# Row sums of a gathered table in one instruction or in two halves, beside GpSimd gathers

## The chip, the cores and the metric

The kernel runs on one core of one Trainium2 chip. The metric is the device time of one execution in microseconds, median of three runs. The profile is one execution taken by the hardware profiler; its times are microseconds from the start of its span.

## The reference

The program is a small language model in float32 for 256 positions of width 1024: a latent-attention layer, a gated-linear-attention layer, each followed by a product-key expert layer ("peer"), and a second block with a convolution, an attention and a mixture of 32 experts. The change touches only the peer layers. For a block of 128 positions each of them does this:

```python
def one_block(xi):                                   # xi: 128 positions x 1024
    q = (xi @ w_query).reshape(B, T, PEER_HEADS, 2, PEER_HALF)
    s = jnp.einsum('bthcd,cnd->bthcn', q, sub_keys).astype(jnp.float32)
    s_top, i_top = lax.top_k(s, PEER_TOPK)           # 16 of 128, twice for each of 8 heads
    ...                                              # the best 16 of the pairs: idx, gate
    u = u_tab[idx]                                   # 8 x 16 rows of 1024 for each position
    h = jax.nn.gelu(jnp.einsum('bthkd,btd->bthk', u, xi).astype(jnp.float32), approximate=False)
    w = (gate * h).astype(xi.dtype)
    return jnp.einsum('bthk,bthkd->btd', w, v_tab[idx])
```

Each position picks 128 rows of the table `u_tab`, and as many of `v_tab`, by the same indices. With two layers and two blocks of positions there are four groups of 128, in all 512 steps that the kernel calls rows: in row n every one of the 128 partitions (positions) has one table row of 1024 numbers of its own.

## The kernel before

A row n goes through five engines. GpSimd issues an indirect DMA (`fetch_u`, L671) that brings the 128 table rows, 512 KB, into one of nine buffers `u_rows`, and another (`fetch_v`, L683) for `v_rows`, also nine buffers. VectorE multiplies the u rows with the normalised activations `px` and sums over the 1024 columns into one column of `hid` (L1025, in `row`); the product itself is written back over the buffer and is not used. The semaphore `u_used` counts these. ScalarE applies gelu to eight columns of `hid` at once (L1522), VectorE multiplies them with the gates (L1033, columns of `wgt`), ScalarE makes of each column of `wgt` a diagonal matrix (L1533), and TensorE multiplies the diagonal with the v rows and adds up in two banks of PSUM (L2005). A last few rows are added by VectorE (L1039).

The order on each engine is written out by hand. `Rows` deals out rows between other work: the stage functions (`mla`, `gla`, `route`) call it at their steps, and a table of row targets says how many rows each engine is to have done by each TensorE job. `row(n)` on VectorE sums row n, and at every eighth row, with an offset of two, asks for the gelu of the eight before: `dve.wait_ge(gelu_ready, n // BLK)`. `row(n)` on ScalarE issues the gelu of a full block of eight, and the diagonal of the row ten before; TensorE follows twelve rows behind (`LAG`). In `route`, VectorE runs the top-k of the next group (L913 to L917, six records for each of sixteen score vectors, then index arithmetic) with rows between. At the same time attention or gated linear attention for the other half of the positions keeps TensorE busy.

GpSimd issues its gathers in one fixed order, u and v by turns. Before u row n it waits until row n - 9 has been summed (`pool.wait_ge(u_used, n - RU + 1)`), before v row n until row n - 9 has been multiplied (`v_used`). So a sum that is late can hold the u gather nine rows on, and all gathers behind it in the queue. Each gather reads its 128 indices from a column of `idx` in SBUF.

The sum at L1025 is one call that becomes two instructions on VectorE: the multiply and sum, and a read of the accumulator into the column of `hid`.

Of the kernel before, what the change touches and what calls it, by code (L numbers as in the profile page):

```python
# [6 lines left out]
P = 128  # L7
# [3 lines left out]
BANK = 512  # L11
# [23 lines left out]
BLK, LAG = 8, 12  # L35
# [179 lines left out]
def summed(n):  # L215

    return n - sum(m < n for m in SHARED)
# [69 lines left out]
def build(nc, a, out):  # L287
    f32, i32, u32 = mybir.dt.float32, mybir.dt.int32, mybir.dt.uint32
    ALU, ACT, AX = mybir.AluOpType, mybir.ActivationFunctionType, mybir.AxisListType
    X = AX.X  # L290
    ctx = ExitStack()
    with ctx:
        def sb(name, shape, dt=f32):
            return ctx.enter_context(nc.sbuf_tensor(name, shape, dt))

        def sem(name):
            return ctx.enter_context(nc.semaphore(name))
# [31 lines left out]
        px = sb("px", [P, 2, D])  # L329
        idx = sb("idx", [P, 2, P], i32)  # L330
        gate = sb("gate", [P, 2, P])
        hid = sb("hid", [P, P])
        gel = sb("gel", [P, P])
        wgt = sb("wgt", [P, P])
        diag = sb("diag", [P, DIAGS, P])
# [125 lines left out]
        u_here = [sem(f"u_here{i}") for i in range(RU)]  # L461
        v_here = [sem(f"v_here{i}") for i in range(RV)]
        u_used = sem("u_used")
        v_used = sem("v_used")
        v_taken = sem("v_taken")
        gelu_ready = sem("gelu_ready")
# [231 lines left out]
        def _(dve):  # L698
# [13 lines left out]
            V_ = nc.vector  # L712
# [304 lines left out]
            def row(n):  # L1017

                if n >= P + LAG and (n - LAG) % P == 0:
                    add_experts((n - LAG) // P - 1)  # L1020
                if n < NU:
                    g, r = n // P, n % P
                    dve.wait_ge(u_here[n % RU], 16 * (n // RU + 1))
                    u = u_rows[:, n % RU, :]
                    V_.tensor_tensor_reduce(out=u, in0=u, in1=px[:, g % 2, :], scale=1.0, scalar=0.0, op0=ALU.mult,  # L1025
                                            op1=ALU.add, accum_out=hid[:, r:r + 1]).then_inc(u_used, 1)
                n -= LAG - LEAD - BLK
                if n >= BLK and n % BLK == 0 and n <= NU:
                    g, r = (n - BLK) // P, (n - BLK) % P
                    c = slice(r, r + BLK)  # L1030

                    dve.wait_ge(gelu_ready, n // BLK)
                    V_.tensor_tensor(wgt[:, c], gel[:, c], gate[:, g % 2, c], ALU.mult).then_inc(wgt_ready, 1)  # L1033
                    if n < NU:
                        return
                    dve.wait_ge(wgt_ready, NU // BLK)
                    for m in SHARED:
                        dve.wait_ge(v_here[m % RV], 16 * (m // RV + 1))
                        V_.scalar_tensor_tensor(h[:, 1, :], v_rows[:, m % RV, :], wgt[:, m % P:m % P + 1], h[:, 1, :],  # L1039
                                                ALU.mult, ALU.add).then_inc(v_taken, 1)  # L1040
                        dve.wait_ge(v_taken, SHARED.index(m) + 1)

            rows_done = Rows(row)

            def add_experts(g):
                t = g % 2

                dve.wait_ge(v_used, summed((g + 1) * P))
                V_.tensor_tensor(h[:, t, :], h[:, t, :], psum[:, 6:8, :].rearrange("p a b -> p (a b)"),
                                 ALU.add).then_inc(experts_added, 1)  # L1050
                dve.wait_ge(experts_added, g + 1)
# [291 lines left out]
        def _(act):  # L1343
# [172 lines left out]
            def row(n):  # L1516

                if n >= BLK and n % BLK == 0 and n <= NU:
                    r = (n - BLK) % P
                    c = slice(r, r + BLK)  # L1520
                    act.wait_ge(u_used, n)
                    A_.activation(gel[:, c], hid[:, c], ACT.Gelu).then_inc(gelu_ready, 1)  # L1522
                n -= LAG - LEAD
                if 0 <= n < NU:
                    if n % BLK == 0:
                        act.wait_ge(wgt_ready, n // BLK + 1)
                    if n in SHARED:
                        return
                    at = summed(n)
                    if at >= DIAGS:  # L1530

                        act.wait_ge(v_used, at - DIAGS + 1)
                    A_.activation(diag[:, at % DIAGS, :], ident[:], ACT.Copy, scale=wgt[:, n % P:n % P + 1]).then_inc(diag_ready, 1)  # L1533

            rows_done = Rows(row)

            def gla(t):
# [772 lines left out]
```

## Time and profile before

| | |
|---|---|
| timed runs | 2536.88, 2541.75, 2551.35 us; median 2541.75 |
| profiled execution | span 2647.6 us, the only time listed for it |
| VectorE, GpSimd busy | 1096.6 us (41%), 1124.9 us (42%) |
| L1025, row sums | 512, 616.4 us, mean 1225 ns |
| L671 and L683, gather issues | 512 each, 566.3 and 554.8 us |
| row sums run | from 152.2 to 1761.8 us |
| gathered data | 536.94 MB of 860.19 MB |

"Busy" is the union of an engine's instruction records; an instruction that waits is not busy. A group in the list of the costliest gives the busy time, the mean duration, and the idle time of the engine just before it with what ended it. For a gather on GpSimd the record is the issue of the DMA, not its transfer. A line of the windows view begins with the stretch and its length; then come the busy time and, in brackets, the number of records of PE, PEld, DVE, ACT and POOL, the granted TensorE clock, the busy share of the DMA engines, and the GB/s that they moved. The timeline gives one line for each instruction: start, length, engine, line, operation, and in square brackets the idle time before it. Records of one engine can overlap by some 0.08 us, since an instruction may begin before the one ahead has quite ended. The profiled span is longer than the timed runs; differences in it are read within the profile.

### The profile page before, as it was taken

The page shows a single profiled execution, that of the slowest core. Times are in us where ns is not written, and L with a number is a line of the kernel's source. Part 1 is how long each engine was busy: PE and PEld are TensorE (multiplying, and loading weights), DVE is VectorE, ACT ScalarE, POOL GpSimd, SP SyncE. Part 2 cuts the span into 40 slices and gives each one's busy share as a digit, 9 for nine tenths or more (in the row PEclk, how much of TensorE's full clock was granted, in tenths as well). Part 3 has the DMA queues.
Part 4 walks back from the last instruction along what each step waited for, and adds up shares of the span by engine and source line. Part 5 has one row for each costly group of instructions (what it writes and reads, how often), then busy time and mean ns, then how long its engine had stood idle before and what let it go on. Part 6 is the DMA issues. An engine that isn't in the chain of part 4 may idle for free.

```text
span 2647.6 us, 21106 instructions
## 1 busy us (share of the span) xinstructions
PE 2024.5 (76%) x7462; PEld 1050.7 (40%) x7462; DVE 1096.6 (41%) x2630; ACT 423.9 (16%) x1107; POOL 1124.9 (42%) x1059
## 2 busy tenths in 40 slices
PE   8937797769888677988775866769999995655664
PEld 5613453325344224434331322225888862222221
DVE  6578538942356764345783544431201230000001
ACT  2312311101311110311110111100112310000000
POOL 0057757775556776565776777750000000000000
PEclk9968899899999899999888999999989997887777
DMA  5379999999989999998999999995653369999996
GB/s 208 112 269 350 341 366 390 360 367 383 381 294 398 357 357 377 397 335 315 363 353 364 355 362 365 362 373 135 146 140 102 132 278 403 426 427 427 427 427 272
DMA packets 228318, 860.19 MB, mean 325 GB/s; under 512 B 26080, under 2 KB 26592, under 8 KB 216432
## 3 DMA queue, kind: packets, MB, share of 16 engines
q0 software_dynamic: 147456, 536.94, 54.0%
q1 hardware_dynamic: 77488, 312.04, 31.2%
q10 hardware_dynamic: 3264, 9.80, 1.0%
q8 instruction: 63, 1.03, 0.2%
q14 instruction: 47, 0.39, 0.0%
HBM read 857.64 MB, written 1.05 MB: 324 GB/s over the span
## 4 chain that ended last, share of the span: by engine, by line
PE 39%; DMA 18%; DVE 17%; POOL 11%; issue 8%; another core or an unknown queue 5%; ACT 2%; SPq 1%; DVEq 0%; ACTq 0%; POOLq 0%
PE psum L1814 12%; PE psum L2005 11%; PE psum L1806 6%; DVE rows L1025 6%; POOL rows L671 5%; POOL rows L683 5%; DMA rows<-in_w_e_gate 5%; DMA rows<-in_peer_v,idx 4%; DMA rows<-in_w_e_down 4%; DMA rows<-in_w_e_up 3%; PE psum L2207 3%; PE psum L2230 1%; SPq L546 1%; DVE work L914 1%
## 5 line engine op out<-in xcount | busy, mean ns | idle before, releaser
L2005 PE MATMUL psum<-rows,diag 128*128 128x512 f32 x2024 | 1009.1, 642 | 375.6 <-ACT diag L1533 168.8
L2005 PEld LDWEIGHTS psum<-rows,diag 128*128 128x128 f32 x2024 | 387.9, 203 | 947.4 <-issue 698.0
L1025 DVE CUSTOM_DVE_ANT_0 rows<-rows,px 128x1024 f32<-128x1024 f32 x512 | 616.4, 1225 | 310.7 <-DMA rows<-in_peer_u,idx 258.7
L671 POOL DMA_INDIRECT rows<-in_peer_u,idx x512 | 566.3, 1106 | 383.6 <-issue 149.0
L683 POOL DMA_INDIRECT rows<-in_peer_v,idx x512 | 554.8, 1084 | 271.7 <-issue 129.3
L1814 PE MATMUL psum<-work,rows 128*128 128x256 f32 (+1 forms) x1664 | 292.8, 337 | 7.9 <-issue 7.1
L1814 PEld LDWEIGHTS psum<-work,rows 128*128 128x128 f32 x1664 | 264.4, 196 | 39.5 <-issue 14.4
L1533 ACT ACTIVATE diag<-ident,wgt 128x128 f32<-128x128 f32 x506 | 167.3, 389 | 397.9 <-DVE wgt L1033 222.4
L2207 PE MATMUL psum<-rows,work 128*32 128x512 f32 x896 | 138.2, 699 | 102.3 <-DMA kept<-in_w_e_up 45.8
L1295 DVE TENSOR_TENSOR work<-kept,psum 128x512 f32<-128x512 f32 x8 | 8.2, 1030 | 426.9 <-PE psum L2207 426.9
L1352 ACT ACTIVATE work<-psum 128x512 f32<-128x512 f32 (+4 forms) x158 | 81.8, 533 | 616.3 <-PE psum L1814 161.1
L1806 PE MATMUL psum<-rows,work 128*128 128x512 f32 x354 | 156.0, 595 | 3.6 <-ACT work L1352 1.9
L694 POOL IOTA work<- 128x256 f32 x1 | 0.3, 345 | 306.4 <-ACT kept L1352 306.4
L2230 PE MATMUL psum<-rows,kept 128*32 128x512 f32 x448 | 75.0, 749 | 71.0 <-DMA kept<-in_w_e_down 40.2
L2207 PEld LDWEIGHTS psum<-rows,work 128*32 128x32 f32 x896 | 39.1, 126 | 195.0 <-issue 194.9
L1806 PEld LDWEIGHTS psum<-rows,work 128*128 128x128 f32 x354 | 67.2, 191 | 88.5 <-issue 85.9
L1522 ACT ACTIVATE gel<-hid 128x8 f32<-128x8 f32 x64 | 13.2, 207 | 437.1 <-DVE hid L1025 269.8
L2207 PE MATMUL psum<-kept,work 128*32 128x512 f32 x128 | 70.7, 716 | 0.0
L2230 PEld LDWEIGHTS psum<-rows,kept 128*32 128x32 f32 x448 | 20.0, 134 | 120.4 <-issue 119.5
L913 DVE MAX8 work<-work 128x8 f32<-128x128 f32 (+1 forms) x96 | 27.4, 285 | 76.5 <-issue 38.1
L1814 PE MATMUL psum<-rows 128*128 128x256 f32 x256 | 58.5, 391 | 0.0
L1352 ACT ACTIVATE rows<-psum 128x512 f32<-128x512 f32 (+3 forms) x49 | 27.2, 565 | 186.9 <-PE psum L1814 107.9
(308 smaller groups left out, 1351.3 us busy)
## 6 DMA issues: line engine op xcount, KB each, us to landing
rows<-in_w_e_up SPq DMA_DIRECT2D x28, 2048.0 KB, 19.6
rows<-in_w_e_gate SPq DMA_DIRECT2D x25, 2048.0 KB, 20.3
rows<-in_w_e_down SPq DMA_DIRECT2D x24, 2048.0 KB, 20.2
rows<-in_w_in SPq DMA_DIRECT2D x32, 1024.0 KB
rows<-in_gla_w_in SPq DMA_DIRECT2D x24, 1024.0 KB
rows<-in_peer_w_query SPq DMA_DIRECT2D x16, 1024.0 KB
rows<-in_peer_u,idx POOLq DMA_INDIRECT x512
rows<-in_peer_v,idx POOLq DMA_INDIRECT x512
```

The costliest lines, as they stand in the source:

```text
L546: eng.dma_start(e_matrix(odd, m, e)[:, :, cs], src[:, :, cs]).then_inc(here or e_w[at % PLACES], 16)
L671: pool.indirect_dma_start(out=u_rows[:, n % RU, :], out_offset=None, in_=a["peer_u"][g // 2], in_offset=bass.IndirectOffsetOnAxis(ap=idx[: ...
L683: pool.indirect_dma_start(out=v_rows[:, n % RV, :], out_offset=None, in_=a["peer_v"][g // 2], in_offset=bass.IndirectOffsetOnAxis(ap=idx[: ...
L913: link(V_.max(vals[:, 0:8], src))
L1025: V_.tensor_tensor_reduce(out=u, in0=u, in1=px[:, g % 2, :], scale=1.0, scalar=0.0, op0=ALU.mult, op1=ALU.add, accum_out=hid[:, r:r + 1]). ...
L1352: A_.activation(dst, src, func, scale=scale)
L1533: A_.activation(diag[:, at % DIAGS, :], ident[:], ACT.Copy, scale=wgt[:, n % P:n % P + 1]).then_inc(diag_ready, 1)
L1806: last = mm(bank[:, 0:cols], lhs(k), rhs(k), start=k == 0, stop=k == kn - 1)
L1814: last = mm(bank[:, i * n:(i + 1) * n], w.at(k)[:, c0:c0 + P], x[:, k, :], start=k == 0, stop=k == KD - 1)
L2005: last = mm(psum[:, 6 + c, :], diag[:, at % DIAGS, :], v_rows[:, n % RV, c * BANK:(c + 1) * BANK], start=r == 0, stop=summed(n + 1) == sum ...
L2207: last = mm(psum[cs, 6 + m, :], e_xT[:, k, cs], e_matrix(odd, m, e)[:, k, :], start=k == 0, stop=k == KD - 1)
L2230: last = mm(psum[cs, 4 + c, :], e_actT[:, j, cs], e_matrix(odd, 2, e)[:, j, c * BANK:(c + 1) * BANK], start=j == 0, stop=j == F // P - 1)
```

## The change

Each row is summed by two instructions of 512 columns, and each half has its accumulator read into its own column of a new buffer `hid_half` (two sets of eight columns). After the eighth row of a block one addition of 128 x 8 elements joins the two sets into `hid`. It waits for the last half sum, and signals a new semaphore `hid_ready`; gelu waits for that in place of `u_used`, and so does the first half sum of the next block, which would otherwise overwrite a column that is still being read. `u_used` is counted by the second half of a row, as before by the whole.

```diff
+        hid_half = sb("hid_half", [P, 2, BLK])
...
+        hid_ready = sem("hid_ready")
...
                     dve.wait_ge(u_here[n % RU], 16 * (n // RU + 1))
                     u = u_rows[:, n % RU, :]
-                    V_.tensor_tensor_reduce(out=u, in0=u, in1=px[:, g % 2, :], scale=1.0, scalar=0.0, op0=ALU.mult,
-                                            op1=ALU.add, accum_out=hid[:, r:r + 1]).then_inc(u_used, 1)
+                    at = n % BLK
+                    if n >= BLK and at == 0:
+
+                        dve.wait_ge(hid_ready, n // BLK)
+                    for c in range(2):
+                        cs = slice(c * BANK, (c + 1) * BANK)
+                        last = V_.tensor_tensor_reduce(out=u[:, cs], in0=u[:, cs], in1=px[:, g % 2, cs], scale=1.0, scalar=0.0,
+                                                       op0=ALU.mult, op1=ALU.add, accum_out=hid_half[:, c, at:at + 1])
+                    last.then_inc(u_used, 1)
+                    if at == BLK - 1:
+                        dve.wait_ge(u_used, n + 1)
+                        V_.tensor_tensor(hid[:, r - at:r + 1], hid_half[:, 0, :], hid_half[:, 1, :], ALU.add).then_inc(hid_ready, 1)
...
-                    act.wait_ge(u_used, n)
+                    act.wait_ge(hid_ready, n // BLK)
                     A_.activation(gel[:, c], hid[:, c], ACT.Gelu).then_inc(gelu_ready, 1)
```

On VectorE, behind the first attention of the second block of positions, this stood around the end of a block of eight rows before (ISA is the sum and its accumulator read; `u_here` is the arrival of the gathered row):

```order
L1025 ISA rows,hid<-rows,px 128x1024 [waits u_here1]
L1025 ISA hid 128x1
L1025 ISA rows,hid<-rows,px 128x1024 [waits u_here2]
L1025 ISA hid 128x1
L785 RECIPROCAL small<-small 128x16 [waits emptied]
L786 TENSOR_TENSOR work<-work,small 128x1024 [waits dve_link]
L1025 ISA rows,hid<-rows,px 128x1024 [waits dve_link,u_here3]
L1025 ISA hid 128x1
L1025 ISA rows,hid<-rows,px 128x1024 [waits u_here4]
L1025 ISA hid 128x1
L1033 TENSOR_TENSOR wgt<-gel,gate 128x8 [waits gelu_ready]
```

Now the same place begins so:

```order
L1033 ISA rows,hid_half<-rows,px 128x512 [waits u_here1]
L1033 ISA hid_half 128x1
L1033 ISA rows,hid_half<-rows,px 128x512
L1033 ISA hid_half 128x1
L1038 TENSOR_TENSOR hid<-hid_half 128x8 [waits u_used]
L1033 ISA rows,hid_half<-rows,px 128x512 [waits hid_ready,u_here2]
L1033 ISA hid_half 128x1
L1033 ISA rows,hid_half<-rows,px 128x512
L1033 ISA hid_half 128x1
L787 RECIPROCAL small<-small 128x16 [waits emptied]
L788 TENSOR_TENSOR work<-work,small 128x1024 [waits dve_link]
L1033 ISA rows,hid_half<-rows,px 128x512 [waits dve_link,u_here3]
```

Every row has four instructions in place of two, the addition stands behind the eighth row, and only the first row behind it has the wait for `hid_ready`. The place of `wgt`, three rows behind the addition, is the same; in the second piece it comes two rows further on. ScalarE has as many instructions in the same order, with the other semaphore at gelu, first before and then after:

```order
L1522 ACTIVATE gel<-hid 128x8 [waits u_used]
L1533 ACTIVATE diag<-ident,wgt 128x128 [waits wgt_ready]
```

```order
L1534 ACTIVATE gel<-hid 128x8 [waits hid_ready]
L1545 ACTIVATE diag<-ident,wgt 128x128 [waits wgt_ready]
```

Nothing moved there. GpSimd's and TensorE's instructions are the same in the same order. All lines behind the addition of the buffer carry numbers that are larger by 1 to 12: L1025 became L1033, L1522 became L1534, L671 and L683 became L673 and L685.

## Rows read from the trace of the kernel before

**Rows 1.** The page: span, and busy time of each engine with its share.

```profile
span 2647.6 us, 21106 instructions
...
PE 2024.5 (76%) x7462; PEld 1050.7 (40%) x7462; DVE 1096.6 (41%) x2630; ACT 423.9 (16%) x1107; POOL 1124.9 (42%) x1059
```

**Rows 2.** The page: the chain that ended last, by line.

```profile
PE psum L1814 12%; PE psum L2005 11%; PE psum L1806 6%; DVE rows L1025 6%; POOL rows L671 5%; POOL rows L683 5%; DMA rows<-in_w_e_gate 5%; DMA rows<-in_peer_v,idx 4%; DMA rows<-in_w_e_down 4%; DMA rows<-in_w_e_up 3%; PE psum L2207 3%; PE psum L2230 1%; SPq L546 1%; DVE work L914 1%
```

**Rows 3.** Windows, all engines, where top-k runs between rows.

```profile
440.00:516.00 76.00, 54.37 (x103) 22.30 (x102) 70.47 (x200) 12.12 (x36) 57.88 (x52) 0.85 0.98 363
...
sum 372.00, PE 259.57 PEld 107.72 DVE 311.90 ACT 55.39 POOL 277.90; mean PE 64.89 PEld 26.93 DVE 77.97 ACT 13.85 POOL 69.48
```

**Rows 4.** Windows, L1025 alone, the sum of the same four stretches.

```profile
sum 372.00, DVE 157.72; mean DVE 39.43
```

**Rows 5.** Windows, all engines, first, last and sum of four other stretches.

```profile
232.00:300.00 68.00, 61.88 (x201) 33.56 (x201) 43.32 (x75) 27.93 (x72) 50.94 (x48) 0.93 0.96 359
...
1380.00:1740.00 360.00, 248.39 (x503) 88.67 (x504) 158.54 (x279) 42.37 (x137) 262.04 (x250) 0.96 0.96 362
sum 584.00, PE 420.30 PEld 168.93 DVE 286.77 ACT 92.86 POOL 432.47; mean PE 105.07 PEld 42.23 DVE 71.69 ACT 23.21 POOL 108.12
```

**Rows 6.** Timeline, 1560 to 1579 us: start, length, instruction, idle before it.

```profile
1560.96 1.16 POOL L683 DMA_INDIRECT rows<-in_peer_v,idx  x1 [0.30 <-issue]
...
1577.10 1.22 DVE L1025 CUSTOM_DVE_ANT_0 rows<-rows,px 128x1024 f32<-128x1024 f32 x1 [2.17 <-DMA rows<-in_peer_u,idx]
1577.28 1.85 POOL L683 DMA_INDIRECT rows<-in_peer_v,idx  x1 [0.30 <-issue]
```

**Rows 7.** Timeline of VectorE, 511 to 518 us.

```profile
511.60 0.16 DVE L1033 TENSOR_TENSOR wgt<-gel,gate 128x8 f32<-128x8 f32 x1
511.68 1.22 DVE L1025 CUSTOM_DVE_ANT_0 rows<-rows,px 128x1024 f32<-128x1024 f32 x1
...
516.47 1.21 DVE L1025 CUSTOM_DVE_ANT_0 rows<-rows,px 128x1024 f32<-128x1024 f32 x1
...
517.61 1.21 DVE L1025 CUSTOM_DVE_ANT_0 rows<-rows,px 128x1024 f32<-128x1024 f32 x1
```

**Rows 8.** Timeline of VectorE, 23 to 59 us, about the sums at L813.

```profile
23.77 0.56 DVE L813 CUSTOM_DVE_ANT_0 work<-work 128x384 f32<-128x384 f32 x1 [1.71 <-ACT work L1352]
...
24.34 0.43 DVE L813 CUSTOM_DVE_ANT_0 work<-work 128x256 f32<-128x256 f32 x1
...
57.33 0.56 DVE L813 CUSTOM_DVE_ANT_0 rows<-rows 128x384 f32<-128x384 f32 x1 [0.19 <-DVE work L863]
...
57.81 0.42 DVE L813 CUSTOM_DVE_ANT_0 rows<-rows 128x256 f32<-128x256 f32 x1
58.16 0.08 DVE L813 DVE_READ_ACCUMULATOR2_ANT small<- 128x1 f32 x1
58.27 0.17 DVE L732 TENSOR_SCALAR small<-small 128x2 f32<-128x2 f32 x1
58.48 0.17 DVE L738 TENSOR_SCALAR small<-small 128x2 int32<-128x2 int32 x1
```

**Rows 9.** The page, costliest groups: busy, mean ns, idle before and its causes.

```profile
L1025 DVE CUSTOM_DVE_ANT_0 rows<-rows,px 128x1024 f32<-128x1024 f32 x512 | 616.4, 1225 | 310.7 <-DMA rows<-in_peer_u,idx 258.7
L671 POOL DMA_INDIRECT rows<-in_peer_u,idx x512 | 566.3, 1106 | 383.6 <-issue 149.0
L683 POOL DMA_INDIRECT rows<-in_peer_v,idx x512 | 554.8, 1084 | 271.7 <-issue 129.3
```

**Rows 10.** Waits: who waited for whom, us in total, times, longest.

```profile
ACT gel L1522 <- DVE hid L1025: 269.8, 28, 25.3
```

**Rows 11.** The line L683: duration in ns, least, median and most.

```profile
L683 POOL DMA_INDIRECT rows<-in_peer_v,idx x512: 935/941/1992, 160.7 to 1779.9; - x171
```

**Rows 12.** Timeline, 468 to 471 us.

```profile
468.86 1.23 DVE L1025 CUSTOM_DVE_ANT_0 rows<-rows,px 128x1024 f32<-128x1024 f32 x1
469.47 1.43 POOL L671 DMA_INDIRECT rows<-in_peer_u,idx  x1 [0.30 <-issue]
```

## The prediction, made before the changed kernel ran

> **What bounds the kernel now.** I read the page first, then the waits, then windows, then the timeline of single instructions. The part of the kernel in question is the 512 row sums at L1025, which run from about 152 to 1762 us of a span of 2647.6 us [rows 1]. In that time no compute engine is full on average: VectorE is busy 1096.6 us in all, GpSimd 1124.9 us [rows 1]. The chain that ended last gives L1025 6%, and 5% to each of the two gather lines [rows 2]. 6% of the span is 159 us, or 130 rows at 1.225 us: about a quarter of the rows are on the chain.
>
> Averages hide that different stretches have different limits, so I cut two groups of windows. In the first (four stretches, where the router's top-k runs between rows) VectorE is busy 311.9 of 372 us, up to 70.5 of 76 [rows 3], and 157.72 us of that are L1025 [rows 4]; with its accumulator read a row takes 1.21 us of busy time, so they are 130 rows, as many as the chain has. I call them VectorE-led. In the second group, 584 us, VectorE is about half idle, and GpSimd is the full one: 432.47 us in 407 gather issues (48, 56, 53 and 250 in the four windows) [rows 5], each with a gap of 0.30 us before it [rows 6] that is not counted as busy. 407 x 0.30 = 122 us, so 554 of 584 us are taken. There the DMA share is 0.96 to 0.98 too [rows 5]: issue and transfer are both within 5% of full. Between the two groups lie the stages of attention and gated linear attention with TensorE work beside the rows; I expect nothing from the change there beyond a microsecond or two.
>
> **The change, part by part.**
>
> 1. Two halves in place of one. Back to back, one row starts 1.14 to 1.15 us after the one before it, although its record lasts 1.21: the accumulator read and the next row begin together, before the first has quite ended [rows 7]. For a half of 512 columns there is no row. Nearest are the same operation with 384 and 256 columns: 384 to its successor 0.48 us, 256 to its read 0.35 us [rows 8]. 0.13 us for 128 columns gives 0.61 us for 512, two halves 1.22 to 1.23 us, so +0.08 us a row. The upper bound comes from the other time that the 384 ran: 23.77 to 24.34, 0.57 us, the read not covered [rows 8]. With 0.09 us on each half it is +0.26 us a row. Below nothing is excluded: the columns are the same and the fixed part is paid twice. I take +0.08, since the row pattern itself shows covered reads.
>
> By the Trainium skill, "VectorE: DVE Perf Modes", section on the DRAIN, the next operation does not start until the pipe is empty, and its rules say to minimise the count of operations. The trace does not agree for this operation (1.14 us from start to start under records of 1.21). By that rule each half would cost its whole record, some 0.69 us, and a row +0.16.
>
> 2. One small addition for eight rows, with a wait before it (the last half must have landed) and one behind it (the next row may overwrite the half sums). The same shape stands at L1033, 0.16 us [rows 7]. Chained small operations on VectorE start 0.20 to 0.21 us apart with 0.17 us of work [rows 8], so a wait on one's own engine costs about 0.04. Sum: 0.08 for the last half's covered end, 0.04, 0.16, 0.04, which is 0.32 us a block, 0.04 us a row. Bounds: 0.08 a block if it is covered as L1033 is (there the row behind it starts 0.08 later [rows 7]), 0.5 if the waits are dearer.
>
> Together +0.12 us a row: 61 us of VectorE over 512 rows. Of this only what falls in VectorE-led stretches is on the path: 130 x 0.12 = 16 us. VectorE idles 60 us in those windows [rows 3], part of it while a row is on its way, and takes back some; I subtract 4. So +12 us. With the upper bound of the halves, 130 x (0.26 + 0.04) = 39 us. The rest lies in idle time: 258.7 us of waiting for gathered rows in all [rows 9].
>
> 3. Gelu waits for the addition, about 0.3 us later. Its product is asked of VectorE only behind three more rows, and a diagonal is due later still. ScalarE waits for the sums 28 times [rows 10]; were each on the path it would be 8 us. I take 1. Queued behind the waiting gelu are the diagonals, for which TensorE waits. On VectorE the row's first half is queued behind the new wait, so u_used and with it GpSimd's next u gather come late by as much; nine buffers cover it except in the VectorE-led stretches, where it is already counted. GpSimd waits 90.6 us for row sums as it is [rows 9].
>
> 4. What nobody added: how long a gather issue is held up. An issue takes 941 ns at the median and up to 1992 ns [rows 11]. The timeline says why. The issue at 469.47 took 1.43 us; a row sum was running from 468.86 and ended at 470.09, and 0.81 us later the issue was done. The issue at 1577.28 met the row sum of 1577.10 to 1578.32, took 1.85 us, and was done 0.81 us behind it [rows 6, 12]. One with no row sum in its way takes the 0.94 of the median. So an issue that meets a row sum waits for that instruction's end. Over 1024 issues that is 566.3 + 554.8 - 1024 x 0.941 = 157 us [rows 9]. A half ends sooner: an issue held for 0.91 us would be held for about 0.38, one held for less than 0.6 us gains nothing. The seven v issues from 1560.96 to 1577.28, whose first and last stand in [rows 6], are held 0.22, 0.14, 0.39, 0.50, 0.07, 0.07 and 0.91 us, 2.30 in all; 0.53 of it, 23%, would go. In the GpSimd-led stretches the hold is 432.5 - 407 x 0.941 = 49.5 us; 23 to 35% off is 11 to 17 us. The DMA engines at 0.96 to 0.98 let at most 3% of 584, 18 us, through. Which of the two binds changes from gather to gather and the rows don't tell, so I take half of 14: -7 us. Bounds 0 and -25 (half of all hold there).
>
> The Trainium skill, "SBUF — State Buffer", section on who interferes with whom, says that a VectorE instruction with two SBUF inputs contends with a GpSimd instruction that reads SBUF, whoever comes first holding it for the whole instruction. The trace agrees, 1.85 against 0.94 us. It adds that descriptor generation was not seen stalled by such operations; here it is. By the first statement step 4 stands, by the second it would be nothing and the sum 5 to 7 us higher.
>
> Sum on the profiled execution: +12 + 1 - 7 = +6 us on a span of 2647.6. The timed median is 2541.75, 4% shorter, so the profile stretches something; scaled, +5 to +6. Forecast 2547 us.
>
> **Rivals.**
>
> A (forecast): small terms of both signs, 2547, its own range 2533 to 2561.
>
> B, slower: the reads are not covered, and the VectorE-led stretches take it all. 39 us and 1 for gelu, less the 4 us of idle: +36, scaled +35: 2577. It decides from about 0.20 us a row on. For it: one of the two records of 384 columns [rows 8]; top-k between rows leaves no slack. Against it: the back-to-back rows.
>
> C, faster: the hold is what paces the gathers, and halves break it. -25 in the GpSimd-led stretches, and in the VectorE-led ones, where the u issues are held for up to 0.5 us [rows 12], their share wins back most of +12: net -22, 2520. For it: 554 of 584 us taken. Against: DMA at 0.96 to 0.98, and most holds shorter than a half.
>
> D, hidden anyway: the DMA engines set the pace through all rows, including the top-k stretches (share 0.98 [rows 3]); the added VectorE time fits in its idle time, and the shorter hold buys nothing: 2542. Against it: VectorE at 70.5 of 76 us in one window cannot take 5% more for nothing.
>
> **How the numbers follow.** A 0.42, B 0.24, C 0.20, D 0.14. What a measurement here can tell from no change is 0.5%, 12.7 us. Faster: C but for 0.02, and 0.03 of A: 0.21. Slower: B but for 0.01, and 0.06 of A: 0.29. Same: 0.50. The range 2522 to 2579 leaves out the outer parts of B and C.
>
> **What would show it.** Two records of about 0.69 us a row, the second 0.61 us behind the first: 0.70 instead would be B. The mean of a gather issue falls from 1.10 to about 1.05 us and the longest from 1.99 to some 1.45 us; if it stays, step 4 is wrong. The top-k stretches grow by some 3 to 4 us each; 232 to 300 and 1380 to 1740 shrink by 1 to 2%. The gathers would end within 10 us of 1782 in the trace of before. A move in the expert stage behind them, or a gap at gelu, would mean a cause I have not named.

## The result and the profile after

The changed kernel takes 2511.48 us (2508.82 to 2518.04, 4 runs), the kernel before 2546.55 us beside it: ratio 0.9876, 95% interval 0.9842 to 0.9911. A second time on another occasion it was 0.9878 (0.9844 to 0.9913). That is 35 us faster by these medians and 31 by the ratio, 11 us under the low end of my range; the forecast had it slower by 5, the likeliest case, no measurable change, was wrong, and the mechanism of rival C happened, larger than I had priced it.

First the page of the kernel after: span, busy time, the chain by line, and the groups that answer to [rows 1, 2, 9] (group, count, busy us, mean ns, idle before).

```profile
span 2507.1 us, 22242 instructions
...
PE 1995.8 (80%) x7462; PEld 1034.6 (41%) x7462; DVE 1152.5 (46%) x3718; ACT 421.9 (17%) x1107; POOL 1032.9 (41%) x1059
...
PE psum L1826 13%; PE psum L2017 9%; DVE rows L1033 8%; POOL rows L685 7%; POOL rows L673 6%; PE psum L1818 5%; DMA rows<-in_w_e_gate 5%; DMA rows<-in_w_e_down 4%; DMA rows<-in_peer_v,idx 4%; DMA rows<-in_w_e_up 3%; PE psum L2219 3%; DMA rows<-in_gla_w_in 2%; PE psum L2242 1%; DVE work L916 1%; SPq L548 1%
...
L1033 DVE CUSTOM_DVE_ANT_0 rows<-rows,px 128x512 f32<-128x512 f32 x1024 | 661.1, 691 | 268.6 <-DMA rows<-in_peer_u,idx 254.3
L673 POOL DMA_INDIRECT rows<-in_peer_u,idx x512 | 517.3, 1010 | 372.8 <-issue 146.2
L685 POOL DMA_INDIRECT rows<-in_peer_v,idx x512 | 511.8, 1000 | 234.3 <-issue 135.5
...
L1033 DVE DVE_READ_ACCUMULATOR2_ANT hid_half<- 128x1 f32 x1024 | 83.1, 81 | 0.0
```

The span, 2507.1 us, agrees with the timed runs. That of before did not (2647.6 against 2546.55), so I had the kernel before profiled once more, unchanged:

> The kernel before, unchanged, for a second profile of it. Its first profile had a span of 2647.6 us while its runs took 2546.55. If the gathers were slow in that one execution for a reason of their own, the span is now near 2547, the gather packets are shorter and the stretch 1380 to 1740 moves about 390 GB/s in place of 362; the time that gather issues are held (157 us there) should stay between 120 and 200 us, since it comes from the overlap with row sums. If the profiler itself slows this kernel, the span is again near 2640.

It ran in 2537.62 us with this page:

```profile
span 2535.8 us, 21106 instructions
...
PE 1994.8 (79%) x7462; PEld 1025.1 (40%) x7462; DVE 1100.9 (43%) x2630; ACT 422.1 (17%) x1107; POOL 1104.3 (44%) x1059
...
L1025 DVE CUSTOM_DVE_ANT_0 rows<-rows,px 128x1024 f32<-128x1024 f32 x512 | 620.1, 1226 | 365.1 <-DMA rows<-in_peer_u,idx 355.1
...
L671 POOL DMA_INDIRECT rows<-in_peer_u,idx x512 | 557.1, 1088 | 353.4 <-issue 149.8
L683 POOL DMA_INDIRECT rows<-in_peer_v,idx x512 | 543.4, 1061 | 210.3 <-issue 128.0
```

The first expectation held (from 1380 to 1560 us it moves 406 GB/s where the first profile moved 356, and gather issues are held 137 us in all). In the execution that I had worked from the gathers were slower than they usually are: in it the last gather starts at 1779.9 us, in the second one at 1667.7, and in the kernel after at 1639.8. So the difference of the two first profiles, 140 us, is not the change. I compare with the second from here on. Windows, all engines (stretch, length, busy us and records of PE, PEld, DVE, ACT, POOL, clock, DMA share, GB/s), of the second profile of before:

```profile
420.00:520.00 100.00, 75.92 (x153) 28.24 (x152) 85.09 (x222) 16.16 (x48) 78.65 (x71) 0.95 1.01 394
820.00:940.00 120.00, 86.03 (x175) 29.39 (x173) 87.51 (x209) 18.01 (x54) 93.77 (x87) 1.00 0.99 378
1260.00:1380.00 120.00, 89.13 (x184) 32.69 (x184) 75.58 (x145) 19.20 (x56) 93.21 (x88) 0.97 1.00 380
1380.00:1560.00 180.00, 136.93 (x276) 46.83 (x276) 85.94 (x147) 22.03 (x75) 137.71 (x139) 1.00 1.02 406
```

and of after:

```profile
420.00:520.00 100.00, 78.75 (x155) 30.79 (x156) 88.16 (x303) 17.05 (x52) 73.09 (x72) 0.91 1.03 409
820.00:940.00 120.00, 94.21 (x193) 37.29 (x194) 96.98 (x322) 19.79 (x60) 92.37 (x91) 0.94 1.02 404
1260.00:1380.00 120.00, 94.93 (x200) 37.35 (x199) 83.17 (x248) 19.99 (x59) 92.27 (x92) 0.94 1.02 399
1380.00:1560.00 180.00, 137.66 (x278) 46.74 (x276) 94.14 (x298) 23.90 (x81) 137.04 (x142) 1.00 1.03 409
```

The last number is the one to read. Where nothing but rows runs (1380 to 1560), both kernels move 406 to 409 GB/s at a share of 1.02 to 1.03. In none of the profiles with a shorter hold does a stretch of 40 us of the gathers go above 410, so I take that for what the DMA engines give here, and there was next to nothing to win. In the three stretches in and behind the top-k the kernel before moved 378 to 394 GB/s and the kernel after 399 to 409.

GpSimd is the full engine in all four of before. From 820 to 940 us its 87 issues are busy 93.77 us, and each has its gap of 0.30 us before it: 120 of 120 us, with no longer wait. At 1.38 us for a gather of 512 KB that is 380 GB/s, and 378 were moved.

The top-k has two parts that must be read apart. In its sweeps over the score vectors (L913 to L917, rows between) VectorE is the full one. The last two sweeps run from 770 to 857 and from 1176 to 1262 us in the second profile of before, and from 766 to 857 and 1162 to 1253 us in that of after. Before:

```profile
770.00:857.00 87.00, 69.23 (x157) 26.65 (x155) 81.47 (x267) 12.37 (x41) 66.09 (x60) 0.98 1.01 393
1176.00:1262.00 86.00, 67.46 (x155) 26.49 (x153) 80.49 (x262) 12.38 (x41) 65.85 (x60) 0.98 0.96 354
```

and after:

```profile
766.00:857.00 91.00, 75.05 (x167) 31.39 (x165) 85.10 (x340) 12.37 (x41) 68.12 (x69) 0.92 1.03 408
1162.00:1253.00 91.00, 74.07 (x167) 31.01 (x165) 85.09 (x339) 12.37 (x41) 68.12 (x69) 0.92 0.99 385
```

Each of the two holds 36 rows and got longer, 86.4 to 91.3 us, but GpSimd gets 69 issues out in it in place of 60. Behind the sweep (first index arithmetic with rows between; 857 to 994 us in the second profile of before) VectorE waits for gathered rows, 50 us in all, and the gathers that were issued early pay there. The start of single row sums, counted out in the two timelines, shows it:

```
row                160   230   280   340   383   415   511
before, second us  620   850   994  1212  1323  1409  1657
after, us          613   850   976  1199  1300  1383  1630
```

27 us are won by the last row. What was won by row 160 (7 us) is given back by row 230, where the sweep at 770 to 857 us ends. 18 are won from row 230 to 280, nearly all behind that sweep; 6 go again by row 340, a good way into the last sweep; 11 come back by row 383, behind it, 3 more by row 415, and none after that. A second execution of the kernel after has the same pattern (+5, -2, +15, +9, +20, +24 and +23 us at these rows).

The cost on VectorE is near the forecast. Timeline of after, start and length, at the end of a block of eight rows:

```profile
167.02 0.68 DVE L1033 CUSTOM_DVE_ANT_0 rows<-rows,px 128x512 f32<-128x512 f32 x1
167.63 0.08 DVE L1033 DVE_READ_ACCUMULATOR2_ANT hid_half<- 128x1 f32 x1
167.63 0.70 DVE L1033 CUSTOM_DVE_ANT_0 rows<-rows,px 128x512 f32<-128x512 f32 x1
168.26 0.08 DVE L1033 DVE_READ_ACCUMULATOR2_ANT hid_half<- 128x1 f32 x1
168.37 0.17 DVE L1038 TENSOR_TENSOR hid<-hid_half 128x8 f32<-128x8 f32 x1
168.46 0.29 DVE L915 MAX8 work<-work 128x8 f32<-128x128 f32 x1
```

A half follows a half after 0.61 us, the value of step 1 (from [rows 8]). The addition moves its successor from 168.26 to 168.46, 0.20 us. That is where top-k follows. Where the next row follows at once and has to wait for the addition it is more:

```profile
790.99 0.07 DVE L1033 DVE_READ_ACCUMULATOR2_ANT hid_half<- 128x1 f32 x1
791.09 0.17 DVE L1038 TENSOR_TENSOR hid<-hid_half 128x8 f32<-128x8 f32 x1
791.40 0.69 DVE L1033 CUSTOM_DVE_ANT_0 rows<-rows,px 128x512 f32<-128x512 f32 x1
```

The row starts at 791.40 where it could have started at 790.99, 0.41 us; my 0.32 lies between the two. The 4.9 us by which a sweep of 36 rows grew are 0.14 us a row, against 0.12 forecast.

The gather issues also did what step 4 says, seen in the same kernel:

```profile
454.46 0.69 DVE L1033 CUSTOM_DVE_ANT_0 rows<-rows,px 128x512 f32<-128x512 f32 x1
454.52 1.44 POOL L673 DMA_INDIRECT rows<-in_peer_u,idx  x1 [0.30 <-issue]
```

The issue at 454.52 met the half that ends at 455.15 and was done at 455.96, 0.81 us behind it, as in [rows 6, 12]. It was held 0.50 us; a whole row sum from 454.46 would, by the same rule, have held it 1.03. Over the whole second profile of before, 322 of the 359 issues that took more than 1.0 us ended 0.79 to 0.83 us behind a row sum; issues that had begun 0.1 to 0.2 us before a row sum were held 0.01 us in the mean. Means fell from 1088 and 1061 ns to 1010 and 1000. Against 0.941 for an issue alone, the time held in all is 137 us before (second profile) and 66 us after. I call this time the hold.

### The profile page after: what moved, and what is told of

The parts are those of the page before. It is cut to its first block, busy times and chain, and to the rows that moved or that the text cites. A ratio compares the mean times of both kernels' runs of the same rounds, so it can differ in the third digit from the quotient of the medians.

```text
span 2507.1 us, 22242 instructions
## 1 busy us (share of the span) xinstructions
PE 1995.8 (80%) x7462; PEld 1034.6 (41%) x7462; DVE 1152.5 (46%) x3718; ACT 421.9 (17%) x1107; POOL 1032.9 (41%) x1059
## 3 DMA queue, kind: packets, MB, share of 16 engines
q8 instruction: 63, 1.03, 0.2%
## 4 chain that ended last, share of the span: by engine, by line
PE 38%; DVE 20%; DMA 20%; POOL 13%; issue 6%; ACT 2%; SPq 1%; DVEq 0%; ACTq 0%
PE psum L1826 13%; PE psum L2017 9%; DVE rows L1033 8%; POOL rows L685 7%; POOL rows L673 6%; PE psum L1818 5%; DMA rows<-in_w_e_gate 5%; DMA rows<-in_w_e_down 4%; DMA rows<-in_peer_v,idx 4%; DMA rows<-in_w_e_up 3%; PE psum L2219 3%; DMA rows<-in_gla_w_in 2%; PE psum L2242 1%; DVE work L916 1%; SPq L548 1%
## 5 line engine op out<-in xcount | busy, mean ns | idle before, releaser
L2017 PE MATMUL psum<-rows,diag 128*128 128x512 f32 x2024 | 990.0, 630 | 267.6 <-ACT diag L1545 155.5
L1033 DVE CUSTOM_DVE_ANT_0 rows<-rows,px 128x512 f32<-128x512 f32 x1024 | 661.1, 691 | 268.6 <-DMA rows<-in_peer_u,idx 254.3
L2017 PEld LDWEIGHTS psum<-rows,diag 128*128 128x128 f32 x2024 | 378.0, 198 | 834.2 <-issue 564.3
L673 POOL DMA_INDIRECT rows<-in_peer_u,idx x512 | 517.3, 1010 | 372.8 <-issue 146.2
L685 POOL DMA_INDIRECT rows<-in_peer_v,idx x512 | 511.8, 1000 | 234.3 <-issue 135.5
L1534 ACT ACTIVATE gel<-hid 128x8 f32<-128x8 f32 x64 | 13.2, 207 | 453.0 <-DVE hid L1038 452.9
L1033 DVE DVE_READ_ACCUMULATOR2_ANT hid_half<- 128x1 f32 x1024 | 83.1, 81 | 0.0
```

Source lines behind the costliest of these rows:

```text
L673: pool.indirect_dma_start(out=u_rows[:, n % RU, :], out_offset=None, in_=a["peer_u"][g // 2], in_offset=bass.IndirectOffsetOnAxis(ap=idx[: ...
L685: pool.indirect_dma_start(out=v_rows[:, n % RV, :], out_offset=None, in_=a["peer_v"][g // 2], in_offset=bass.IndirectOffsetOnAxis(ap=idx[: ...
L1033: last = V_.tensor_tensor_reduce(out=u[:, cs], in0=u[:, cs], in1=px[:, g % 2, cs], scale=1.0, scalar=0.0, op0=ALU.mult, op1=ALU.add, accum ...
L2017: last = mm(psum[:, 6 + c, :], diag[:, at % DIAGS, :], v_rows[:, n % RV, c * BANK:(c + 1) * BANK], start=r == 0, stop=summed(n + 1) == sum ...
```

## Experiments

Each was timed against the kernel before on the same chip. Theory H: a gather issue waits for the end of a row sum, because that has two inputs in SBUF, and this kept the gathers below what the DMA engines can do. Theory J: the gain comes from gelu's later release. Theory K: some other trait of the summing instruction holds the issues.

**The join alone.** Whole row sums, with the small addition and its waits.

```diff
-                    for c in range(2):
-                        ... accum_out=hid_half[:, c, at:at + 1])
+                    last = V_.tensor_tensor_reduce(out=u, in0=u, in1=px[:, g % 2, :], ..., accum_out=hid_half[:, 0, at:at + 1])
...
-                        ... hid_half[:, 0, :], hid_half[:, 1, :], ALU.add).then_inc(hid_ready, 1)
+                        ... hid_half[:, 0, :], zeros[:, 0:BLK], ALU.add).then_inc(hid_ready, 1)
```

> Whole row sums of 1024 columns as before, but each into a buffer of eight, with the small addition (to zeros), the wait before it, gelu released by it, and the first row of a block waiting for it: part 2 of the change alone. Theory H: no gain from this, only 0.04 us a row: 2545 to 2558. Theory J (release of gelu): it takes the gain of the change with it, 2510 to 2525.

Measured 2550.61 us, ratio 1.0032 (1.0004 to 1.006). J falls: the part of the change that it needs costs time when it is alone.

**One input in place of two.**

```diff
-                    V_.tensor_tensor_reduce(out=u, in0=u, in1=px[:, g % 2, :], ..., accum_out=hid[:, r:r + 1]).then_inc(u_used, 1)
+                    V_.tensor_reduce(hid[:, r:r + 1], u, X, ALU.add).then_inc(u_used, 1)
```

> The row sum leaves out the product with the activations: it is one reduction of 1024 columns of the gathered row, one input from SBUF in place of two, no write of the product, no second instruction for the accumulator; everything else as in the kernel before (the numbers differ, so later layers pick other rows, and the expert stage may differ; the stretch up to the last gather is what counts). Theory H: VectorE is busy as long as before for a row (1.2 us) but no gather issue is held by it: issues at 0.94 us nearly all, held time under 20 us, the last gather at or before that of the halves, time 2495 to 2515. Theory J or any that leaves the second input out: held time as before, 120 to 160 us, time 2535 to 2550.

Measured 2495.99 us, ratio 0.9815 (0.9759 to 0.9871). Its gather issues, and two of its windows:

```profile
L683 POOL DMA_INDIRECT rows<-in_peer_v,idx x512 | 487.0, 951 | 267.7 <-PE psum L2004 144.0 <-issue 123.1 <-DVE hid L1025 0.6
L671 POOL DMA_INDIRECT rows<-in_peer_u,idx x512 | 486.7, 951 | 378.5 <-DVEq L708 146.2 <-issue 123.2 <-DVE hid L1025 109.0
```

```profile
820.00:940.00 120.00, 90.41 (x187) 32.75 (x186) 88.52 (x159) 18.52 (x55) 91.05 (x95) 0.97 1.03 409
1260.00:1380.00 120.00, 93.76 (x196) 35.25 (x196) 68.53 (x79) 21.86 (x65) 90.72 (x97) 0.97 1.03 409
```

The hold is gone (951 ns, 10 us in all over 0.941), these stretches run at 409 GB/s, and the time is 45 us less though VectorE is busy 1.22 us a row as before. But the write of the product and the accumulator read went too, so the input isn't yet named as the cause.

**Two inputs without the sum.**

```diff
+                    if n == 0:
+                        V_.memset(hid[:], 1.0)
+                    V_.tensor_tensor(u, u, px[:, g % 2, :], ALU.mult).then_inc(u_used, 1)
```

(in place of the row sum of the kernel before)

> The row sum leaves out the summing: one tensor_tensor product of 1024 columns, two inputs from SBUF, the product written back, no accumulator and no second instruction; hid is a constant (later layers pick other rows, and the expert stage may differ: the stretch up to the last gather counts). Theory H (the second SBUF input holds the gather issues): held time 120 to 160 us, as with the whole row sum, and a time near the kernel before, 2530 to 2550. Theory K (the summing form or its accumulator read holds them, not the second input): held time under 30 us, time like that of the one-input reduction, 2490 to 2505.

Measured 2541.89 us, ratio 0.9995 (0.9969 to 1.0021), with these issues:

```profile
L671 POOL DMA_INDIRECT rows<-in_peer_u,idx x512 | 559.1, 1092 | 354.0 <-issue 149.4 <-DVEq L708 145.4 <-DVE rows L1027 59.2
L683 POOL DMA_INDIRECT rows<-in_peer_v,idx x512 | 550.2, 1075 | 207.3 <-issue 124.9 <-PE psum L2006 82.4
```

1092 and 1075 ns, 146 us held, and the time is that of the kernel before: as with the whole sum. Neither summing nor the accumulator read matters; K falls in that form. The product is still written back here, and the one-input kernel wrote none, so the write is left as a cause until the next pair, which keeps it.

**The second input in PSUM.** The whole computation, with TensorE's other work in four banks in turn instead of six, and the activations in the two freed banks. First the base:

```diff
-NB = 6
+NB = 4
```

> The kernel before with four in place of six PSUM banks in turn for TensorE's other work, so that two banks are free: the base for the next kernel. Both theories: no faster, 2540 to 2560.

Measured 2535.23 us, ratio 0.9985 (0.9954 to 1.0016): the two banks cost nothing that can be measured. Then:

```diff
+                    px_banks = psum[:, 4:6, :].rearrange("p a b -> p (a b)")
+                    if r == 0:
+                        if g:
+                            dve.wait_ge(u_used, n)
+                        link(V_.tensor_copy(px_banks, px[:, g % 2, :]))
-                    V_.tensor_tensor_reduce(out=u, in0=u, in1=px[:, g % 2, :], scale=1.0, scalar=0.0, op0=ALU.mult,
+                    V_.tensor_tensor_reduce(out=u, in0=u, in1=px_banks, scale=1.0, scalar=0.0, op0=ALU.mult,
```

> Whole row sums of 1024 columns as before, with the activations in the two freed PSUM banks (copied there by VectorE at the first row of each of the four groups): one input from SBUF, the other from PSUM, all of the computation kept. Theory H: no gather issue is held (held time under 20 us), VectorE pays neither for halves nor for a join: against the kernel with four banks -30 to -45 us, 2500 to 2515 in all, and as good as or better than the changed kernel. Theory K (what holds the issues is the form of the summing instruction): held time as before and no gain, 2540 to 2560.

Measured 2499.40 us (2497.30 to 2499.61), ratio 0.9827 (0.9784 to 0.9869). It is 36 us below its base, as expected. This is the best kernel of the study that computes everything, 12 us ahead of the changed one; they ran on different occasions, but the ratios point the same way, 0.9827 against 0.9878, though their intervals overlap. Its groups, a stretch of its timeline and two windows:

```profile
L1030 DVE CUSTOM_DVE_ANT_0 rows<-rows,psum 128x1024 f32<-128x1024 f32 x512 | 614.8, 1219 | 287.5 <-DMA rows<-in_peer_u,idx 276.4 <-DVE small L775 1.1 <-DVE work L1089 0.7
L671 POOL DMA_INDIRECT rows<-in_peer_u,idx x512 | 488.2, 953 | 376.9 <-DVEq L708 144.6 <-issue 124.8 <-DVE hid L1030 107.5
L683 POOL DMA_INDIRECT rows<-in_peer_v,idx x512 | 484.9, 947 | 273.7 <-PE psum L2010 148.1 <-issue 125.3 <-DVE hid L1030 0.3
```

```profile
1500.20 1.22 DVE L1030 CUSTOM_DVE_ANT_0 rows<-rows,psum 128x1024 f32<-128x1024 f32 x1 [1.33 <-DMA rows<-in_peer_u,idx]
1500.81 0.94 POOL L671 DMA_INDIRECT rows<-in_peer_u,idx  x1 [0.31 <-issue]
```

```profile
820.00:940.00 120.00, 91.66 (x185) 32.80 (x183) 90.88 (x210) 17.92 (x54) 91.02 (x96) 0.97 1.03 409
1260.00:1380.00 120.00, 93.75 (x197) 34.90 (x196) 71.33 (x130) 19.88 (x59) 90.90 (x96) 0.97 1.03 409
```

The issue at 1500.81 begins 0.61 us into a row sum of the same form and the same length as before, and takes 0.94 us: it is done 0.33 us behind the sum's end, not 0.81. The one at 469.47 in [rows 12] also began 0.61 us into its row sum. All that changed for the instruction is where one input lies; the product is still written back, so the write isn't the cause either, and H is what is left. This is the plainest pair in the study: 1.43 us with both inputs in SBUF, 0.94 with one in PSUM.

**What splitting costs, without holds.** The one-input reduction in halves, and in quarters, both with the join.

```diff
-                        last = V_.tensor_tensor_reduce(out=u[:, cs], in0=u[:, cs], in1=px[:, g % 2, cs], ...)
+                        last = V_.tensor_reduce(hid_half[:, c, at:at + 1], u[:, cs], X, ALU.add)
```

> The one-input reduction (the product is left out) in two halves of 512 columns with the join of the change: VectorE pays for the splitting, and no gather issue is held either way. Against the whole one-input reduction (2496) this measures the price of the splitting alone: by the measured 0.08 us a row and 0.20 a block, on about 130 rows, +10 to +14 us under theory H, 2505 to 2512, about level with the changed kernel. If splitting had a merit of its own beside the holds, it would not be slower than 2496.

Measured 2499.68 us, ratio 0.984 (0.9803 to 0.9876): 4 us above the one whole reduction (6 by the ratios, whose intervals overlap), not 10 to 14. Against the one-input halves, the changed kernel (2511.66) has 12 us more. Most of that is probably what its remaining 66 us of hold still cost, but the product and the accumulator reads are also in it; no run takes them apart.

> The one-input reduction (the product is left out) in four pieces of 256 columns with the join, beside the quarters of the whole sum that took 2531 where halves took 2511. If that loss is the VectorE time of splitting, it is here too: 2499.7 for one-input halves, so 2510 to 2525. If it comes from how pieces and gather issues meet, this one stays near 2500.

(the same edit with four pieces) Measured 2513.00 us, ratio 0.9879 (0.9836 to 0.9922). The first splitting costs 4 us, the second 13.

**Quarters of the whole row sum.**

```diff
-                    for c in range(2):
-                        cs = slice(c * BANK, (c + 1) * BANK)
+                    for c in range(4):
+                        cs = slice(c * (D // 4), (c + 1) * (D // 4))
```

(and a reduction over four sets of eight in place of the addition)

> Each row sum in four pieces of 256 columns, joined by one small reduction for eight rows. Theory H (a gather issue that meets a row sum waits for that instruction's end, and this paced the gathers): holds get shorter once more, total held time from 66 us (halves) to 25 to 40 us; but the halves already let the DMA engines run at 409 GB/s behind 1380 us, so little is left to win there, and VectorE pays 2 x 0.08 us more for a row, about 21 us where top-k runs beside: 2515 to 2530, behind the halves. Theory J (the gain comes from when gelu is released, not from the holds): same as the halves but for the VectorE time, 2525 to 2535.

Measured 2531.21 us, ratio 0.9955 (0.993 to 0.9979), 20 us behind the halves and 1 us beyond the worst that I had expected under H. The time lies in the range that I had given J, but J had fallen with the join alone. The mean issue fell little more, to 995 and 992 ns, which is 54 us held; 25 to 40 were expected. Two windows of it, which answer to those above:

```profile
820.00:940.00 120.00, 92.92 (x179) 37.80 (x180) 107.90 (x538) 18.80 (x57) 87.20 (x88) 0.87 1.00 385
1260.00:1380.00 120.00, 97.45 (x200) 39.84 (x199) 100.11 (x491) 19.99 (x59) 89.90 (x89) 0.90 0.99 386
```

VectorE is busy 107.9 and 100.1 of 120 us, each of the last two sweeps takes 97 us where halves took 91, and the gathers are back at 385 GB/s: now VectorE sets the pace behind the sweeps too. 13 of the 20 us are the splitting itself, by the pair before; the other 7 I can't name.

**Once more the changed kernel, and the join later or not at all.**

> The changed kernel, unchanged, timed beside the three others on the same chip. Both theories: 0.985 to 0.990 of the kernel before, about 2511.

Measured 2511.66 us, ratio 0.9878 (0.9844 to 0.9913).

```diff
+                if n >= BLK and n % BLK == 0 and n <= NU:
+                    side, r = (n // BLK - 1) % 2 * 2, (n - BLK) % P
+                    dve.wait_ge(u_used, n)
+                    V_.tensor_tensor(hid[:, r:r + BLK], hid_half[:, side, :], hid_half[:, side + 1, :], ALU.add).then_inc(hid_ready, 1)
```

(behind the row sum of the next block's first row; the half sums go to `side + c`)

> Halves as in the change, but the small addition of a block stands behind the first row of the next block, with two sets of half sums in turn: no instruction has to end before the addition starts, and no row waits for it. Gelu is released one row later. If the 0.20 us that a block's addition takes in the changed kernel are on the path where top-k runs between rows (about 16 blocks there), it is 1 to 3 us faster than the changed kernel; if the release of gelu is what counts, it is slower by up to 64 x 1.3 us times the share of blocks for which ScalarE waits. I expect -2 us, 2505 to 2515.

Measured 2514.37 us, ratio 0.9899 (0.9862 to 0.9935): 3 us more where I had expected 2 less; the intervals overlap, so neither a gain nor a loss is shown.

```diff
+                    for c, sums in ((0, hid_first), (1, hid)):
+                        cs = slice(c * BANK, (c + 1) * BANK)
+                        last = V_.tensor_tensor_reduce(out=u[:, cs], in0=u[:, cs], in1=px[:, g % 2, cs], ..., accum_out=sums[:, r:r + 1])
+                    last.then_inc(u_used, 1)
```

> Halves as in the change, with no join: the second half's accumulator goes to hid itself, gelu waits for u_used as before, the first half's sum is left out of the result (later layers pick other rows). What remains open is the price of the join: join_only took 2550.6 against 2541.1. If the join costs that much beside halves too, this one takes 2502 to 2507; if its 0.20 us a block is all (about 16 blocks on the path, 3 us), 2507 to 2512, level with the changed kernel within the measurement.

Measured 2508.47 us, ratio 0.9875 (0.9836 to 0.9913). By the medians the join costs 3 us beside halves, by the ratios less than 1. The traces are for the 3: each of the last two sweeps lasts 89.9 us without the join and 91.3 with it. Why it cost more by itself (2550.6) stays open; that interval reaches down to 1 us.

## Why the prediction was wrong

**Step 1, the price of the halves.** Right in itself: 0.61 us, two records of 691 ns. The accumulator read is covered, and rival B falls. The Trainium skill's rule on the DRAIN ("VectorE: DVE Perf Modes"), weighed there at +0.16 us a row, is not what this kernel shows: half follows half 0.08 us before its record ends. The same section adds that a next operation that is not held starts earlier, which I had passed over; with that the 0.08 us agree.

**Step 2, the share of it on the path.** Right in place and about in size, too large in the end. I put 130 rows at 0.12 us on the path, less 4: +12 us, 1 more for gelu. The sweeps are VectorE-led as I said (81.5 of 87 us and 80.5 of 86), and the last two grew by 4.9 us each; the one before them did not (90 us both). That is +10. But the one-input pair, where no hold is in play, shows sweeps longer by 3.5 us each and only 4 us at the end. The error was small, and it was in which stretches I called VectorE-led: in the first profile the sweeps end at 219, 488, 920 and 1338 us, so 107 of my 372 us lie behind them, and there VectorE waits for rows (in the second profile it was busy 75.6 of 120 us from 1260 to 1380).

**Step 4, the hold.** This is the step that failed, by size. Its mechanism was right: the 0.81 us, the release at the end of a half. But I priced it at -7 us, at most -25, with the words that the DMA engines at 0.96 to 0.98 let at most 3% through. Measured: -31 us for the change with 4 to 10 us of splitting in it, so some -35 to -41 us for the hold that halves remove; and for nearly all of it -36 us from four banks to the input in PSUM (2535.23 to 2499.40) and -45 us with one input (2541.09 to 2495.99).

Three terms of the step were too small. First, the cap of 3%. The share of busy DMA engines is no distance to a limit when the packets themselves take longer: from 1380 to 1560 us the first profile showed a share of 0.95 at 356 GB/s, the second 1.02 at 406. Had I asked for the highest rate anywhere in the gather stage, the page's own digits (390 GB/s in one slice, 398 in another) stood against it. Second, the share of the hold that halves remove: I took 23 to 35%, and 137 to 66 us is 52%. Third, the rows on which it counts: I gave the hold nothing in the windows that I had called VectorE-led. But in a sweep GpSimd gets 69 issues out in place of 60, and behind the sweep it issues without a wait; there the hold was worth most, 18 us from row 230 to 280. The longest of my own stretches, 1380 on, was at its cap already and gave nothing.

Of the signs that I had named, the two records of 0.69 us, 0.61 us apart, came. The last two sweeps grew by a little more than the 3 to 4 us, the two before them did not. The mean issue fell from 1.075 us (second profile) to 1.005, more than the 0.05 of the forecast. The longest issue stayed at 1.98 us and not 1.45: it met another instruction of VectorE with 1024 columns (L751), which the change doesn't cut. The last gather came 28 us earlier, not within 10.

By the first statement of the Trainium skill's page "SBUF — State Buffer" (a VectorE instruction with two SBUF inputs contends with a GpSimd instruction that reads SBUF) the hold had to be there; the runs bear it out, with one input (951 ns) as with PSUM (953 and 947). Its note that such operations were not seen to stall descriptor generation doesn't hold here: 1092 ns with the plain two-input product against 951.

**The rivals.** C had 0.20 and 2520 us; its case (the hold paces the gathers, halves break it) happened with 8 us more than its net -22. What I held against it, the DMA share, was the misread number. D was right that the DMA engines cap the gathers, but it had stretches at the cap that were not (378 GB/s against 409).

**The warning that I passed over.** The profile's span, 4% longer than the median of the timed runs, was no matter of scale. I wrote that "the profile stretches something" and went on to take bounds from just the rows that were stretched.

## What to carry to other kernels

Beside a queue of GpSimd gathers, look at the mean time of a gather issue in each stretch and at which VectorE instructions with two SBUF inputs it meets, not at VectorE's load: in this kernel an issue that began beside one waited for its end. Where GpSimd issues without a wait, cut such instructions in two if VectorE has idle time (-31 us here), and better, put one input in PSUM if banks are free, which cost VectorE nothing here (1219 ns a row against 1226) and gave -36. When a profile's span isn't the timed runs', take no cap from it before a second one.

## What the hardware showed that I had not expected

- Of what these runs varied in an instruction of 1024 columns, only the place of its inputs made the hold: two in SBUF, summing or not, 1061 to 1106 ns a mean issue; one in PSUM, 947 and 953; one input alone, 951. The bare issue is 0.94 us, and a held one ends 0.81 us behind the instruction it met. So the hold depends on when the issue begins: in the second profile of before, issues that began some 0.3 us into a row sum were held 0.77 us in the mean, those at 0.6 us 0.49, those at 0.9 us 0.19.
- The gathers of 512 KB reach 409 GB/s on this core and no more: behind the sweeps in the kernels without holds, and in the kernel after from 1380 us on.
- One and the same kernel moved 356 GB/s from 1380 to 1560 us in one profiled execution and 406 in another. What made the first slow stays open; the timed runs of the kernel before lie between 2527 and 2559 us, none near its 2647.6.
